# Cached-key scores run head by head between the query projections, and a full 128-row tile in the expert gather

## The chip, the cores and the metric

One core of a Trainium2 chip runs one program. The metric is the device time of one execution in microseconds (us). TensorE is called PE below, VectorE DVE, ScalarE ACT, GpSimd POOL, and SyncE SP; SP issues the loads of the weights.

## What is computed

One inference step of a two-layer decoder trunk, for a prompt of 256 positions and for 8 samples of one position each, with shared weights. Each layer has a mixing part (causal pooling and a gated recurrence), a cross-attention of 4 heads of width 256 into 256 memory tokens, and a channel mixer: a dense SwiGLU in layer 0, the best two of 8 experts in layer 1. All data is float32. The two parts that the change touches are

```
def mem_attend(xn, k, v, wq, wo):
    q = (xn @ wq).reshape(B, T, MEM_HEADS, MEM_HEAD_DIM)
    s = jnp.einsum('bthd,bmhd->bhtm', q, k).astype(jnp.float32) * (MEM_HEAD_DIM ** -0.5)
    p = jax.nn.softmax(s, axis=-1).astype(xn.dtype)
    o = jnp.einsum('bhtm,bmhd->bthd', p, v).reshape(B, T, D_MODEL)
    return o @ wo

def moe(x, router_w, wg, wu, wd):
    ...
    for e in range(N_EXPERTS):
        out = out + combine[:, e:e + 1] * swiglu(xt, wg[e], wu[e], wd[e])
```

The prompt attends to keys and values that are computed in the step from its own memory and written out. Each of the 8 samples attends to cached keys and values of its own, which have to be read from HBM: per layer 8 samples x 4 heads x 256 tokens x 256 numbers for the keys, 8 MB, and as much for the values.

## The kernel before

The five engines run programs written out by hand, kept in step by semaphores. Activations stand with the model dimension on the partitions, prompt and samples side by side: 264 columns, of which 256 are the prompt's and the last 8 the samples'.

**The stream of units.** Weights and cached keys and values come in units of 128 x 1024 numbers, 512 KB each, in the order that `stream_plan` lists. SP loads unit k into slot k modulo 8 of a ring of eight slots, in that order, as soon as the slot is free (L522). A weight unit is split: ACT writes its high part (`high_part`, L993), DVE subtracts it from the raw unit for the low part (`low_part`, L1370) and so frees the slot; three buffers hold split units. A product of weights and activations is three matmuls (high with high, high with low, low with high; L587 to L589), and `project_pair` does two output tiles of 128 with two units, 48 matmuls. Raw units (kinds `kc`, cached keys, and `vc`, cached values) are not split: PE reads them straight from the ring, and a matmul on PE frees their slot (`frees`). In each layer the order is: `in`, `mk`, `mv`, `out`, `kn`, then the 8 query units `mq`, the 16 `kc`, the 16 `vc`, the 8 units `mo` of the attention's output projection.

**The attention** on PE runs in this order: all query projections; the prompt's scores for two halves t of the prompt and two pairs hp of heads (L712); the samples' scores (L724); the transposes of the prompt's probabilities (L735); the prompt's values, eight tiles (L748); the transpose of the samples' probabilities (L754); the samples' values (L764); the transpose of their outputs (L773); then `mo`. A sample has one query column, so the kernel keeps a zeroed array `qz` with eight columns per chunk and sample, of which only the sample's own is filled: a matmul with these 8 columns as its stationary side and a sample's keys as its moving side adds to that sample's row and nothing to the others. Four such matmuls, one per head, write four groups of 32 output partitions (the row of head h and sample b is 32 h + b). The values use an array `pz` of the same kind. DVE takes the maxima (L1545, L1558), ACT the exponentials with their sums, DVE divides (L1551 to L1562) and copies the turned sample probabilities into `pz` (L1572). DVE zeroes `qz` and `pz` in each layer (L1527, L1528). A unit of the caches holds one head of two samples. The sample scores run in four quarters of four units, the four heads of one pair of samples each, and so do the sample values.

**The expert part.** `gather` multiplies the tokens (three tiles of 128, 128 and 8 rows, `TOK`; high and low parts, L848 and L849) with selection matrices to collect each expert's tokens: four times in all, once per pair of experts, 48 matmuls each. `turn_scatter` transposes an expert's selection matrix in the same three pieces (L858).

POOL copies the small outputs, and issues the write-out of the prompt's keys and values (L1829, L1833).

Of the kernel before, what the change touches and what calls it, by code (L numbers as in the profile page):

```python
# [18 lines left out]
ALU = mybir.AluOpType  # L19
# [86 lines left out]
def stream_plan():  # L106
# [22 lines left out]
def bank_plan():  # L129

    out = []
    for l in range(DEPTH):
# [17 lines left out]
        out += [("sc", l, t, hp) for t in range(2) for hp in range(2)]  # L150
        out += [("scs", l)]
        out += [("pt", l, h) for h in range(NH)]
        out += [("pv", l, m) for m in range(KC)]
        out += [("pts", l)]
        out += [("pvs", l)]
# [16 lines left out]
def trunk_kernel(nc, xT, memT, vecs, taps, hists, consts, pool_w, gate_w, router_w, dense, experts,  # L172
# [51 lines left out]
    with ExitStack() as ctx:  # L224
# [63 lines left out]
        STAGE = 3 * NH * NM + NH * MC * TP + KC * TS * TS + NH * MC * TS * TS  # L288
# [17 lines left out]
        pr = take(3 * NH * NM).rearrange("p (t h m) -> p t h m", t=3, h=NH)  # L306
        prs = pr[:, 2, 0, :]
# [98 lines left out]
        kv_written = sem("keys_values_written")  # L406
        qz_ready = sem("sample_queries_ready")
# [6 lines left out]
        mask_ready = sem("mask_ready")  # L414
        route_ready = sem("route_ready")
# [156 lines left out]
        def _(pe):  # L572
# [76 lines left out]
            for l in range(DEPTH):  # L649
# [50 lines left out]
                project("mq", l, xhi, xlo, T, xn_ready, KC * (3 * l + 1))  # L700

                for m in range(KC):
                    wait_read(pe, tiles[key_tile(l, m)])
                    wait_read(pe, tiles[("mq", l, m)])
                for t in range(2):
                    for hp in range(2):
                        n = tiles[("sc", l, t, hp)]
                        b = take_bank(n)
                        for hh in range(2):
                            h = 2 * hp + hh  # L710
                            for c in range(HC):
                                i = mm(b[:, hh * NM:(hh + 1) * NM], q[:, HC * h + c, t * P:(t + 1) * P], kT[:, HC * h + c, :],  # L712
                                       start=(c == 0), stop=(c == HC - 1))
                        full(i, n)

                pe.wait_ge(qz_ready, l + 1)
                n = tiles[("scs", l)]
                b = take_bank(n)
                for bp in range(4):
                    w = [raw_unit(("kc", l, 4 * h + bp)) for h in range(NH)]  # L720
                    for b2 in range(2):
                        for c in range(HC):
                            for h in range(NH):
                                i = mm(b[32 * h:32 * h + TS, 0:NM], qz[:, HC * h + c, 2 * bp + b2, :], w[h][:, 2 * b2 + c, :],  # L724
                                       start=(bp + b2 + c == 0), stop=(bp == 3 and b2 + c == 2))
                                if b2 + c == 2 and bp + h < 6:
                                    frees(i, ("kc", l, 4 * h + bp))
# [1233 lines left out]
```

## Time and profile before

| | |
|---|---|
| median of 3 runs | 1230.55 us (1226.32 to 1233.48) |
| profiled execution, device time | 1220.12 us |
| its span in the profile | 1218.3 us |
| PE busy | 1111.4 us (91%) |
| DVE, ACT busy | 795.8 us, 645.7 us |
| moved by DMA | 273.00 MB, mean 224 GB/s |

Busy time of an engine counts the time in which at least one of its instructions ran. Matmuls overlap on PE, so a matmul's own duration is longer than the step from one to the next. A float32 matmul on raw data is two records in the trace. The granted clock is the share of 2.4 GHz that the throttle let TensorE have; 0.50 is 1.2 GHz. "Idle before" is the time an engine stood still ahead of an instruction, and behind the arrow stands what ended it. All times of the trace count from the start of the span.

### The profile page before, as it was taken

The page shows a single profiled execution, that of the slowest core. Times are in us where ns is not written, and L with a number is a line of the kernel's source. Part 1 is how long each engine was busy: PE and PEld are TensorE (multiplying, and loading weights), DVE is VectorE, ACT ScalarE, POOL GpSimd, SP SyncE. Part 2 cuts the span into 40 slices and gives each one's busy share as a digit, 9 for nine tenths or more (in the row PEclk, how much of TensorE's full clock was granted, in tenths as well). Part 3 has the DMA queues.
Part 4 walks back from the last instruction along what each step waited for, and adds up shares of the span by engine and source line. Part 5 has one row for each costly group of instructions (what it writes and reads, how often), then busy time and mean ns, then how long its engine had stood idle before and what let it go on. Part 6 is the DMA issues. An engine that isn't in the chain of part 4 may idle for free.

```text
span 1218.3 us, 19957 instructions
## 1 busy us (share of the span) xinstructions
PE 1111.4 (91%) x7698; PEld 1027.6 (84%) x7698; DVE 795.8 (65%) x1125; ACT 645.7 (53%) x864; POOL 15.0 (1%) x34
## 2 busy tenths in 40 slices
PE   6998996599999998998966789999999999999995
PEld 5998983399999998998943778998989898989984
DVE  5689641275655555787621464886888688868883
ACT  5675541255433445675421334775767476666762
POOL 0001000000000000010000000000000000000000
PEclk9999998699999999999988876999999999999998
DMA  8443457845555554544647333995989598959861
GB/s 326 155 157 126 164 199 297 313 147 181 185 178 187 174 190 132 171 142 150 223 164 291 137 150 117 347 360 207 346 302 372 192 365 289 361 202 362 306 261 38
DMA packets 64276, 273.00 MB, mean 224 GB/s; under 512 B 7328, under 2 KB 7584, under 8 KB 63552
## 3 DMA queue, kind: packets, MB, share of 16 engines
q1 hardware_dynamic: 62352, 264.33, 61.2%
q0 software_dynamic: 1408, 7.12, 1.6%
q8 instruction: 58, 0.95, 0.3%
q10 hardware_dynamic: 432, 0.38, 0.1%
q14 instruction: 26, 0.21, 0.1%
HBM read 265.83 MB, written 5.98 MB: 223 GB/s over the span
## 4 chain that ended last, share of the span: by engine, by line
PE 71%; DVE 14%; ACT 6%; DMA 4%; issue 3%; SPq 1%; DVEq 0%; ACTq 0%
PE bank L590 10%; PE bank L587 10%; PE bank L592 10%; PE bank L591 10%; PE bank L588 10%; PE bank L589 10%; DMA ring<-dense 4%; DVE wl L1370 3%; PE bank L848 2%; ACT wh L993 2%; DVE rstd L1365 2%; PE bank L615 1%; DVE wl L1621 1%; DVE sq L1381 1%; PE bank L748 1%
## 5 line engine op out<-in xcount | busy, mean ns | idle before, releaser
L1621 DVE TENSOR_TENSOR wl<-ring,wh 128x1408 fp32r<-128x1408 f32 x192 | 310.2, 1624 | 60.4 <-ACT wh L1237 60.2
L1370 DVE TENSOR_TENSOR wl<-ring,wh 128x1024 fp32r<-128x1024 f32 x170 | 206.9, 1223 | 215.7 <-ACT wh L993 215.3
L1237 ACT ACTIVATE wh<-ring 128x1408 fp32r<-128x1408 f32 x189 | 261.0, 1381 | 85.9 <-PE bank L592 85.6
L587 PE MATMUL bank<-xh,wh 128*128 128x264 f32 x928 | 271.6, 293 | 19.0 <-DVE xl L1386 14.7
L993 ACT ACTIVATE wh<-ring 128x1024 fp32r<-128x1024 f32 x170 | 178.8, 1056 | 190.0 <-PE bank L589 143.4
L588 PE MATMUL bank<-xl,wh 128*128 128x264 f32 x928 | 267.3, 288 | 0.0
L589 PE MATMUL bank<-xh,wl 128*128 128x264 f32 x928 | 266.6, 287 | 0.0
L591 PE MATMUL bank<-wh,xl 128*128 128x352 f32 (+4 forms) x736 | 243.9, 331 | 0.0
L587 PEld LDWEIGHTS bank<-xh,wh 128*128 128x128 f32 x928 | 178.6, 192 | 25.6 <-issue 21.4
L588 PEld LDWEIGHTS bank<-xl,wh 128*128 128x128 f32 x928 | 179.1, 193 | 0.0
L589 PEld LDWEIGHTS bank<-xh,wl 128*128 128x128 f32 x928 | 178.3, 192 | 0.0
L590 PE MATMUL bank<-wh,gathered_hi 128*128 128x352 f32 x512 | 167.4, 327 | 2.1 <-DVE xl L1699 1.7
L592 PE MATMUL bank<-wl,gathered_hi 128*128 128x352 f32 x512 | 165.1, 322 | 0.0
L591 PEld LDWEIGHTS bank<-wh,xl 128*128 128x128 f32 x736 | 139.4, 189 | 5.7
L590 PEld LDWEIGHTS bank<-wh,gathered_hi 128*128 128x128 f32 x512 | 96.8, 189 | 3.9 <-issue 2.3
L592 PEld LDWEIGHTS bank<-wl,gathered_hi 128*128 128x128 f32 x512 | 96.7, 189 | 0.0
L587 PE MATMUL bank<-hidden_hi,wh 128*128 128x264 f32 (+1 forms) x304 | 86.6, 285 | 1.6 <-DVE hidden_lo L1398 1.4
L588 PE MATMUL bank<-hidden_lo,wh 128*128 128x264 f32 (+1 forms) x304 | 86.0, 283 | 0.0
L589 PE MATMUL bank<-hidden_hi,wl 128*128 128x264 f32 (+1 forms) x304 | 85.7, 282 | 0.0
L590 PE MATMUL bank<-wh,xh 128*128 128x512 f32 (+3 forms) x224 | 80.0, 357 | 0.0
L592 PE MATMUL bank<-wl,xh 128*128 128x512 f32 (+3 forms) x224 | 79.1, 353 | 0.0
L587 PEld LDWEIGHTS bank<-hidden_hi,wh 128*128 128x128 f32 x304 | 57.2, 188 | 2.4 <-issue 2.3
(217 smaller groups left out, 1370.1 us busy)
## 6 DMA issues: line engine op xcount, KB each, us to landing
ring<-experts SPq DMA_DIRECT2D x192, 704.0 KB, 5.9
ring<-dense SPq DMA_DIRECT2D x234, 512.0 KB, 3.8
o_k<-kv POOLq DMA_DIRECT2D x2, 1024.0 KB, 4.4
o_v<-kv POOLq DMA_DIRECT2D x2, 1024.0 KB, 7.7
x<-xT SPq DMA_DIRECT2D x2, 528.0 KB, 4.9
o_y<-sq SPq DMA_DIRECT2D x4, 264.0 KB, 2.1
gatew<-gate_w POOLq DMA_DIRECT2D x2, 512.0 KB, 8.3
mem<-memT SPq DMA_DIRECT2D x1, 1024.0 KB, 13.3
```

The costliest lines, as they stand in the source:

```text
L587: mm(out, s_hi, m_hi, start=start, stop=False)
L588: mm(out, s_hi, m_lo, start=False, stop=False)
L589: return mm(out, s_lo, m_hi, start=False, stop=stop)
L590: mm(out, s_hi, m_hi, start=start, stop=False)
L591: mm(out, s_lo, m_hi, start=False, stop=False)
L592: return mm(out, s_hi, m_lo, start=False, stop=stop)
L848: mm(out, tokh[0:rows, t, f0:f0 + P], slots, start=(t == 0), stop=False)
L993: A(wh[:, k % NBUF, 0:UNIT], raw(u), ACT.Copy).then_inc(hi_ready, 1)
L1237: A(wh[:, jj % NBUF, :], eraw(jj % ESLOTS), ACT.Copy).then_inc(ehi_ready, 1)
L1365: link(V.reciprocal(rstd[:, buf, 0:width], rms[:, buf, 0:width]))
L1370: V.tensor_tensor(wl[:, k % NBUF, 0:UNIT], raw(u), wh[:, k % NBUF, 0:UNIT].bitcast(F32), ALU.subtract)\
L1621: V.tensor_tensor(wl[:, jj % NBUF, :], eraw(jj % ESLOTS), wh[:, jj % NBUF, :].bitcast(F32), ALU.subtract)\
```

## The change

1. `stream_plan`: the four `kc` units of a head follow the query pair that comes after the head's own, in place of all 16 behind the queries.
2. `sample_scores(h)`: the sample scores run per head. `qz` has 32 columns per chunk and sample (head h's sample b fills column 8 h + b of its 32), and the four matmuls that go to the four partition groups are the four pairs of samples, with one unit each; one bank collects all heads. `qz` now lies where the turned prompt probabilities `pT` are written later. DVE signals `qz_ready` once per head.
3. The prompt's scores run by pair of heads, with head 3's sample scores between the pairs; softmax steps on DVE and ACT follow that order (the semaphore values change with it).
4. The samples' probabilities are turned ahead of the prompt's; the first two quarters of the sample values run between the transposes of the prompt's head pairs, the last two behind the prompt's values. Ahead of the copy of the sample outputs DVE splits one unit of `mo`, where it split three.
5. POOL zeroes `qz` and `pz`, when the mixed parts are ready.
6. `gather` and `turn_scatter` use all 128 rows of the third token tile; POOL zeroes that tile once, in layer 1.

```
@@ stream_plan @@
-        for kind, n in (("in", 12), ("mk", 2 * KEYS_FIRST[l]), ("mv", 8), ("out", 8), ("kn", 2), ("mq", 8)):
+        for kind, n in (("in", 12), ("mk", 2 * KEYS_FIRST[l]), ("mv", 8), ("out", 8), ("kn", 2)):
             add(kind, l, n)
-        for kind in RAW:
-            out += [(kind, l, 4 * h + bp) for bp in range(4) for h in range(NH)]
+        for s in range(NH):
+            out += [("mq", l, 2 * s), ("mq", l, 2 * s + 1)]
+            if s > 0:
+                out += [("kc", l, 4 * (s - 1) + bp) for bp in range(4)]
+        out += [("kc", l, 4 * (NH - 1) + bp) for bp in range(4)]
+        out += [("vc", l, 4 * h + bp) for bp in range(4) for h in range(NH)]
...
@@ buffers @@
-        pT = take(NH * MC * TP).rearrange("p (h c t) -> p h c t", h=NH, c=MC)
-        qz = take(KC * TS * TS).rearrange("p (c b s) -> p c b s", c=KC, b=TS)
+        turned = take(NH * MC * TP)
+        pT = turned.rearrange("p (h c t) -> p h c t", h=NH, c=MC)
+        qz = turned.rearrange("p (c b s) -> p c b s", c=KC, b=TS)
...
@@ PE @@
-                project("mq", l, xhi, xlo, T, xn_ready, KC * (3 * l + 1))
...
+                def sample_scores(h):
+                    pe.wait_ge(qz_ready, NH * l + h + 1)
+                    n = tiles[("scs", l)]
+                    b = take_bank(n) if h == 0 else bank(n)
+                    w = [raw_unit(("kc", l, 4 * h + bp)) for bp in range(4)]
+                    for b2 in range(2):
+                        for c in range(HC):
+                            for bp in range(4):
+                                i = mm(b[32 * bp:32 * bp + 32, 0:NM], qz[:, HC * h + c, 2 * bp + b2, :], w[bp][:, 2 * b2 + c, :],
+                                       start=(h + b2 + c == 0), stop=(h == NH - 1 and b2 + c == 2))
+                                if b2 + c == 2 and h + bp < 6:
+                                    frees(i, ("kc", l, 4 * h + bp))
+                    if h == NH - 1:
+                        full(i, n)
...
+                for s in range(NH):
+                    project_pair("mq", l, s, xhi, xlo, T, xn_ready if s == 0 else None, KC * (3 * l + 1))
+                    if s > 0:
+                        sample_scores(s - 1)
+                prompt_scores(0)
+                sample_scores(NH - 1)
+                prompt_scores(1)
...
+                pe.wait_ge(p_ready, 5 * l + 3)
+                for mc in range(MC):
+                    i = nc.tensor.transpose(b[:, mc * P:(mc + 1) * P], prs[:, mc * P:(mc + 1) * P], ident)
                 full(i, n)
+                for h in (0, 1):
+                    prompt_probs(h)
+                pe.wait_ge(pz_ready, l + 1)
+                sample_values(0)
+                sample_values(1)
+                for h in (2, 3):
+                    prompt_probs(h)
...
+                for m in range(KC):
+                    prompt_values(m)
+                sample_values(2)
+                sample_values(3)
...
-                            slots = gsel[0:rows, t, :, :].rearrange("p b s -> p (b s)")
-                            mm(out, tokh[0:rows, t, f0:f0 + P], slots, start=(t == 0), stop=False)
-                            i = mm(out, tokl[0:rows, t, f0:f0 + P], slots, start=False, stop=(t == 2))
+                            slots = gsel[:, t, :, :].rearrange("p b s -> p (b s)")
+                            mm(out, tokh[:, t, f0:f0 + P], slots, start=(t == 0), stop=False)
+                            i = mm(out, tokl[:, t, f0:f0 + P], slots, start=False, stop=(t == 2))
...
-                for t, (t0, rows) in enumerate(TOK):
-                    i = nc.tensor.transpose(b[:, t0:t0 + rows], wsel[0:rows, t, :], ident[0:rows, 0:rows])
+                for t in range(3):
+                    i = nc.tensor.transpose(b[:, t * P:(t + 1) * P], wsel[:, t, :], ident)
...
@@ ACT @@
+            act.wait_ge(tail_zeroed, 2)
...
@@ DVE @@
-                dve.wait_ge(small_staged, 6 * (l + 1))
-                step(V.memset(qz, 0.0))
-                step(V.memset(pz, 0.0))
...
+                dve.wait_ge(qz_zeroed, l + 1)
                 for c in range(KC):
+                    h = c // HC
                     wait_read(dve, tiles[("mq", l, c)])
-                    step(V.tensor_copy(qz[:, c, :, :].rearrange("p b s -> p (b s)")[:, 0:64:TS + 1], q[:, c, TP:T]))
-                    if c % 2:
+                    step(V.tensor_copy(qz[:, c, :, :].rearrange("p b s -> p (b s)")[:, TS * h:TS * h + 232:33], q[:, c, TP:T]))
+                    if c % HC == HC - 1:
+                        signal(qz_ready)
                         S.upto(behind("mq", l, c, 5, start("mo", l)))
...
-                S.upto(start("mo", l) + 3)
+                S.upto(start("mo", l) + 1)
...
@@ POOL @@
+                pool.wait_ge(mixed_ready, KC * (l + 1))
+                G.memset(turned, 0.0).then_inc(qz_zeroed, 1)
+                G.memset(pz, 0.0).then_inc(pz_zeroed, 1)
...
+            wait_full(pool, tiles[("kn", DEPTH - 1, 1)])
+            G.memset(tokh[:, 2, :].bitcast(F32), 0.0).then_inc(tail_zeroed, 1)
+            G.memset(tokl[:, 2, :].bitcast(F32), 0.0).then_inc(tail_zeroed, 1)
```

For two engines the order now and before, as the program holds it. PE in layer 0, from the last query matmul to the first of `mo`, before (`ring` is a raw unit, `work` holds `qz`, `pz` and the probabilities, `sq` the queries, `kv` the prompt's keys and values, `con` the identity; the shape is that of the output):

```order
L589 MATMUL bank<-xh,wl 128x264
L712 MATMUL bank<-kv,sq 128x256 x16
L724 MATMUL bank<-ring,work 8x256 x64
L735 MATMUL bank<-con,work 128x128 x16
L748 MATMUL bank<-work,kv 128x256 x16
L754 MATMUL bank<-con,work 128x128 x2
L764 MATMUL bank<-ring,work 8x256 x64
L773 MATMUL bank<-con,work 128x128 x2
L587 MATMUL bank<-xh,wh 128x264
```

and the same place in the changed kernel:

```order
L597 MATMUL bank<-xh,wl 128x264
L716 MATMUL bank<-ring,work 32x256 x16
L733 MATMUL bank<-kv,sq 128x256 x8
L716 MATMUL bank<-ring,work 32x256 x16
L733 MATMUL bank<-kv,sq 128x256 x8
L783 MATMUL bank<-con,work 128x128 x2
L745 MATMUL bank<-con,work 128x128 x8
L764 MATMUL bank<-ring,work 8x256 x32
L745 MATMUL bank<-con,work 128x128 x8
L754 MATMUL bank<-work,kv 128x256 x16
L764 MATMUL bank<-ring,work 8x256 x32
L803 MATMUL bank<-con,work 128x128 x2
```

The sample scores (L724, now L716) stand in pieces of one head, two more of which lie further ahead between the query pairs, and the sample values (L764 in both) in two halves around the prompt's values (L748, now L754).

DVE in layer 0, in the changed kernel, from the division of the prompt's first head pair to the copy for the sample values (L1593 to L1597 are the sample's softmax, L1574 and L1575 the maxima of the second head pair, L1608 the copy into `pz`):

```order
L1584 TENSOR_SCALAR work<-work,small 128x256 x2
L1593 TENSOR_REDUCE small<-bank 128x1
L1594 TENSOR_SCALAR small<-small 128x1
L1596 RECIPROCAL small<-small 128x1
L1597 TENSOR_SCALAR work<-work,small 128x256
L1574 TENSOR_REDUCE small<-bank 128x2
L1575 TENSOR_SCALAR small<-small 128x2
L1574 TENSOR_REDUCE small<-bank 128x2
L1575 TENSOR_SCALAR small<-small 128x2
L1608 COPY work<-bank 128x4x8 x2
L1581 RECIPROCAL small<-small 128x2
```

Before, the sample's softmax came behind all divisions of the prompt, and the copy into `pz` behind the eight subtractions that follow the prompt's values.

## Rows read from the trace of the kernel before

**Rows 1.** The page, part 2: granted clock in 40 slices of 30.5 us, in tenths.
```profile
PEclk9999998699999999999988876999999999999998
```
**Rows 2.** Windows: stretch, its length, busy time (and instructions) of PE, PEld, DVE, ACT, POOL, clock, DMA share, GB/s.
```profile
148.40:172.60 24.20, 23.16 (x181) 22.01 (x180) 11.58 (x22) 10.82 (x20) 2.15 (x4) 1.00 0.72 272
172.60:234.17 61.57, 36.91 (x341) 21.91 (x341) 15.58 (x41) 13.74 (x34) 0.00 (x0) 0.81 0.71 263
...
615.50:678.90 63.40, 37.01 (x341) 21.83 (x341) 15.54 (x40) 13.68 (x34) 0.00 (x0) 0.81 0.69 257
...
728.68:745.40 16.72, 15.03 (x48) 11.38 (x49) 6.99 (x17) 2.39 (x4) 0.00 (x0) 0.50 0.25 86
745.40:1218.00 472.60, 452.10 (x2608) 417.05 (x2608) 375.91 (x371) 306.63 (x292) 0.00 (x0) 0.99 0.78 282
```
**Rows 3.** Timeline of PE, layer 0: start, length, instructions, count [idle before <- what ended it].
```profile
179.76 3.64 PE L724 MATMUL bank<-ring,work 128*8 128x256 f32 x64
190.71 3.51 PE L724 MATMUL bank<-ring,work 128*8 128x256 f32 x32 [7.31 <-DMA ring<-dense]
195.76 1.91 PE L724 MATMUL bank<-ring,work 128*8 128x256 f32 x32 [1.54 <-DMA ring<-dense]
...
199.65 7.14 PE L748 MATMUL bank<-work,kv 128*128 128x256 f32 x32
...
208.04 3.64 PE L764 MATMUL bank<-ring,work 128*8 128x256 f32 x64 [1.02 <-DVEq L1348]
218.88 3.60 PE L764 MATMUL bank<-ring,work 128*8 128x256 f32 x32 [7.20 <-DMA ring<-dense]
223.90 3.60 PE L764 MATMUL bank<-ring,work 128*8 128x256 f32 x32 [1.42 <-DMA ring<-dense]
232.37 0.66 PE L773 MATMUL bank<-con,work 128*128 128x128 f32 x2 [4.87 <-DVE work L1582]
```
**Rows 4.** Waits in layer 1 (590 to 682): total us, times, longest us.
```profile
PE bank L764 <- DMA ring<-dense: 9.6, 2, 8.2
PE bank L724 <- DMA ring<-dense: 9.4, 2, 8.0
```
**Rows 5.** Windows of 5 us, columns as in rows 2.
```profile
175.00:180.00 5.00, 5.00 (x31) 4.05 (x33) 3.44 (x11) 2.04 (x8) 0.00 (x0) 1.00 0.00 0
180.00:185.00 5.00, 3.40 (x64) 1.52 (x56) 2.61 (x10) 1.93 (x8) 0.00 (x0) 1.00 0.40 143
...
660.00:665.00 5.00, 1.63 (x16) 0.64 (x20) 0.00 (x0) 0.00 (x0) 0.00 (x0) 0.50 1.02 411
```
**Rows 6.** Line L522, the ring's loads: issue to landing.
```profile
DMA to landing us min/median/max: 3.3/3.8/16.4
```
**Rows 7.** Timelines of ACT and DVE, layer 0, columns as in rows 3.
```profile
229.57 1.06 ACT L993 ACTIVATE wh<-ring 128x1024 fp32r<-128x1024 f32 x1 [1.12 <-DMA ring<-dense]
...
199.25 0.35 DVE L1562 TENSOR_SCALAR work<-work,small 128x256 f32<-128x256 f32 x1
...
230.66 1.23 DVE L1370 TENSOR_TENSOR wl<-ring,wh 128x1024 fp32r<-128x1024 f32 x1 [0.95 <-ACT wh L993]
```
**Rows 8.** Timeline of PE in the second gather, start to the instruction behind it.
```profile
833.76 0.36 PE L848 MATMUL bank<-xh,hidden_hi 128*128 128x256 f32 x1 [0.70 <-DVE x L1693]
...
834.19 0.28 PE L849 MATMUL bank<-xh,hidden_lo 128*128 128x256 f32 x1
834.40 0.38 PE L848 MATMUL bank<-xh,hidden_hi 8*128 8x256 f32 x1
834.63 0.27 PE L849 MATMUL bank<-xh,hidden_lo 8*128 8x256 f32 x1
...
842.50 0.55 PE L877 MATMUL bank<-con,work 128*128 128x128 f32 x3
```
**Rows 9.** Timeline of PE, the first expert's matmuls behind the first gather.
```profile
745.43 0.63 PE L590 MATMUL bank<-wh,gathered_hi 128*128 128x352 f32 x1 [1.72 <-DVE xl L1699]
...
750.26 0.38 PE L591 MATMUL bank<-wh,xl 128*128 128x352 f32 x1
```

More of the change, by code:

```diff
@@ L713, in _, with prompt_probs @@
                                        start=(c == 0), stop=(c == HC - 1))
+                                if hp + hh + t + c == 1 and hp == 1:
+                                    frees(i, ("kc", l, 15))
                         full(i, n)
[L716 to L727, printed above, removed]
-                full(i, n)
-                for h in range(NH):
+                def prompt_probs(h):
                     n = tiles[("pt", l, h)]
@@ L749, in _, with sample_values @@
                     full(i, n)
[L750 to L759 removed]
+                def sample_values(bp):
+                    n = tiles[("pvs", l)]
+                    b = take_bank(n) if bp == 0 else bank(n)
                     w = [raw_unit(("vc", l, 4 * h + bp)) for h in range(NH)]
@@ L1159, in _ @@
                                 i.then_inc(exp_done, 1)
-                n = tiles[("scs", l)]
-                act.wait_ge(max_ready, 5 * l + 5)
-                read(A(prs, bank(n)[:, 0:NM], ACT.Exp, bias=nmx[:, 8:9], scale=HD ** -0.5, accum_out=sm[:, 8:9]), n)
+                    if hp == 0:
+                        n = tiles[("scs", l)]
+                        act.wait_ge(max_ready, 5 * l + 3)
+                        read(A(prs, bank(n)[:, 0:NM], ACT.Exp, bias=nmx[:, 8:9], scale=HD ** -0.5, accum_out=sm[:, 8:9]), n)
                 for h in range(NH):
@@ new lines, in normalize @@
+                def normalize(t, hp):
+                    j = 4 * t + 2 * hp
+                    dve.wait_ge(exp_done, 4 * l + 2 * hp + t + 1)
+                    wait_read(dve, tiles[("sc", l, t, hp)])
+                    link(V.reciprocal(rs[:, j:j + 2], sm[:, j:j + 2]))
+                    for hh in range(2):
+                        h = 2 * hp + hh
+                        step(V.tensor_scalar(pr[:, t, h, :], pr[:, t, h, :], rs[:, j + hh:j + hh + 1], None, ALU.mult))
+                    signal(p_ready)
@@ L1556, in _ @@
+                for t in range(2):
+                    top(t, 0)
+                for t in range(2):
+                    normalize(t, 0)
                 n = tiles[("scs", l)]
@@ L1578, in _ @@
                 signal(pz_ready)
-                S.upto(start("mo", l) + 3)
+                for t in range(2):
+                    normalize(t, 1)
+                for m in range(KC):
+                    n = tiles[("pv", l, m)]
+                    dve.wait_ge(oh_ready, KC * l + m + 1)
+                    read(V.tensor_tensor(xlo[:, m, 0:TP], bank(n)[:, 0:TP], xhi[:, m, 0:TP].bitcast(F32), ALU.subtract), n)
+                S.upto(start("mo", l) + 1)
                 n = tiles[("pvs", l)]
```

95 lines of the change are left out of this document (40 added, 55 removed).

## The prediction

> **What bounds the kernel now.** I read the page's slices first: the granted TensorE clock is full almost everywhere and dips in three places [rows 1], the seventh and eighth slice (the attention of layer 0), the twenty-first to twenty-third (that of layer 1), and the two behind, where tokens are routed and gathered. Outside these places PE is near 90% busy, so what PE does in them sets the time. Then the busy time by stretch [rows 2]: from the first prompt score to the first output projection, layer 0 takes 61.57 us of which PE works 36.91, layer 1 takes 63.40 with 37.01. The four query projections ahead of it fill their 24.20 us (23.16 busy, so 5.8 us for a pair of tiles of 48 matmuls, 0.121 each), and in them the DMA moves only 272 GB/s.
>
> The timeline of PE shows where the idle time lies [rows 3]. The sample scores (L724) run their first half in 3.64 us, then PE waits 7.31 us for a load of the ring, runs a quarter, waits 1.54, runs the last. The sample values (L764) do the same: 3.64 us, then waits of 7.20 and 1.42. At the end there is a wait of 4.87 us until DVE has copied the sample outputs. In layer 1 the waits on loads in the same places sum to 9.4 and 9.6 us [rows 4]. Why the loads are late is in the windows [rows 5]: between 175 and 180 us, while PE does prompt scores, the DMA moves nothing. The ring has eight slots, all of them hold raw cache keys, and none is given back before the sample scores, which come last. When they come, half of sixteen units are there and the other half has to stream, at up to 411 GB/s, with PE standing still. The waits also cost clock: it is 1.00 while the first 64 narrow matmuls run and 0.50 in the window 660 to 665, after the wait, so that a quarter takes 3.5 to 3.6 us in place of 1.9 [rows 3, 5].
>
> **The attention, part by part.** The change puts each head's four key units behind the next query pair, so the sample scores of one head (16 matmuls, 32 records, 1.9 us at full clock by the last row of scores) free four slots in the middle of the projections. The loads then run beside 23 us of projections. The sample values are split around the prompt's, which take 7.14 us [rows 3], so that the second half of the value cache loads beside them.
>
> Removed in layer 0: waits 7.31 + 1.54 + 7.20 + 1.42 = 17.5 us, and the half-clock excess of the quarters behind them, (3.51 - 1.85) + 2 x (3.60 - 1.82) = 5.2 us [rows 3]; 22.7 us. Layer 1: 9.4 + 9.6 = 19.0 [rows 4], with the same excess 24.3. Together 47.0 us.
>
> New waits, per layer. (a) The query units of the last pair now stand in the queue behind the second head's keys, in slots that only the first head's scores give back. From there a load lands in 3.8 us [rows 6], two units more lie ahead of it (512 KB at 411 GB/s is 1.28 us each), then ACT (1.06) and DVE (1.23) split it [rows 7], with some 0.3 us of hand-over: 9.0 us, while PE has a pair and one head's scores to do, 5.8 + 1.9 = 7.7. A wait of 1.3. If the queue moves only the 272 GB/s of that stretch (1.93 us a unit), because the prompt's keys and values are written out at the same time, it is 2.6. Bounds 0 (the loads are on time) and about 4 (both ends slip, and the second unit too); I take 2.5, near the busy queue. (b) The sample probabilities need DVE (reduce, exp on ACT, scale): 2.0 us from the last score at 197.6 to the end of the scale at 199.6 [rows 3, 7]. Behind that, DVE now takes two maxima of the second head pair before it may copy the turned probabilities. PE has the second pair's prompt scores and some transposes to cover it. Today PE waits 1.02 us on DVE in that place [rows 3]. Bounds are 0 and 3 (the softmax wholly bare, and 1 us of copy and hand-over); I take 1.3, near the row of today, so 0.3 on top. (c) The last four value units load in slots that the second quarter frees; eight loads in 3.8 + 7 x 1.28 = 12.8 us, while PE has 1.9 + 1.0 + 7.1 + 1.9 = 11.9 from the first quarter's end: 1.3 us with its hand-over, bounds 0 and 3. (d) The tail stays. The first output-projection unit uses the slot of the third quarter of the values, as before, so the 4.87 us (and what follows it) is not won: DVE must split that unit before it copies the sample outputs. It waits for one unit now and not three, but the matmuls ahead are faster, so less lies in front of it; I take 0.5 more, between -3 and 2. Sum of (a) to (d): 2.5 + 0.3 + 1.3 + 0.5 = 4.6 a layer, 9.2 in all.
>
> The two memsets of 512 columns leave DVE for POOL, which waits for the mixed parts and is idle there; cover: the output projection and the key pair that lie between the mixing and the first query copy, over 20 us. Nothing on the path. POOL's key write-out stands behind them, but waits for the last keys anyway. The score matmuls have 32 stationary columns where they had 8. I put the longer weight load at nothing: one of 128 columns already hides behind each matmul of a query pair.
>
> Each change between full and narrow matmuls costs. A full matmul of 256 columns needs 0.117 us (0.121 x 256/264). In the gather at full clock the first 8-row one starts 0.21 after its neighbour, and the second 0.23 after that; a group of six needs 1.09 us (8.74/8) against 0.70 [rows 8]. That is at most 0.38 for one trip into the other shape and back. The attention makes two such trips per layer now and will make six: eight more, 2.9 us at 0.36. The Trainium skill's TensorEngine Tiling, section Key Properties, says that a change of tiling mode drains the engine. This speaks against the attention's new order and for the gather's; the trace agrees, and priced without it the sum would be 2.9 us better in the attention.
>
> Net attention: 47.0 - 9.2 - 2.9 = 34.9 us.
>
> **The gather.** Its last third of tokens is eight rows; the change runs it as 128 with zeros. Three gathers at full clock take 8.74 us each from the first matmul to the one behind [rows 8]; 48 matmuls at 0.117 and a start of 0.1 are 5.7. PE is on the path there (95% busy between 745 and 1218) [rows 2], so 3 x 3.0 = 9.0 us. The first gather is different: it runs from 728.68 to 743.7 (745.43 less the wait of 1.72) wholly at 1.2 GHz [rows 2, 9], and the expert matmuls behind it start at that clock, 0.30 us a step for 16 steps, until at 750.26 they shorten [rows 9]. Without holes 48 steps of 0.30 x 256/352 = 0.22 are 10.5 us at 1.2 GHz: 4.5 won. If the clock rises behind a like unbroken run (745.43 to 750.26 there), 22 steps pass at 0.22 and 26 at 0.117, 7.9 us: 7.1 won, and 16 x (0.30 - 0.16, the same at full clock) = 2.2 behind it, so 9.3. I take 9.3, since the unbroken expert row is the nearest; 4.5 is the other end. The eight transposes of the 8-row piece make trips of the same sort, 0 to 0.36 each less a longer transpose; I take 1.0 for all. The zeroing is POOL's and lies far ahead. Sum 19.3 us.
>
> **The sum.** 34.9 + 19.3 = 54.2 us off. The profiled execution, span 1218.3 and 1220.1 in all, would take 1165.9. The runs shown have a median of 1230.55, 10.4 above it, so I take the difference off the median: 1176 us.
>
> **The rivals.** *A, the loads stay the bound* (they only wait elsewhere). Layer 0's stretch from 148.4 on must pass eleven key and query units, 5.8 MB, beside the outputs that share the 6.6 MB moved there today [rows 2]; and each is held back by a slot. If every head waits 3 us, the attention gains some 17 less: 1193. For it: eight slots for six units per head. Against: the DMA stands idle at 175 to 180 us. The Trainium skill's DMA: Bandwidth & Descriptors, section Specifications, puts the HBM limit at about 358 GB/s per core; by it a unit takes 1.46 us, (a) and (c) grow by some 1.6 a layer, and the time would be 1179. The trace does not agree: 411 GB/s over 5 us [rows 5], so I keep its rate.
>
> *B, slower: the narrow matmuls take the clock.* Between projections they may not hold 2.4 GHz, and then the whole stage from the first query pair on runs at 1.2. PE's work there is 23.2 + 4 x 1.9 + 36.9 less the 5.2 of excess and the old scores' 7.2, some 55 us; doubled it is 110, against 86 now, and the tail of 6 comes on top: 30 us a layer lost, 60 - 19 = 41 in all, 1271. It decides when over half of that stage falls to 1.2 GHz. Against it: the clock is 1.00 in 180 to 185, with x64 narrow records in it [rows 5]; it fell in waits.
>
> *C, the holes in the gather are not the 8 rows'.* Then the second part gives nothing: 1196. Against: in every group the wide steps stand at the 8-row matmuls and directly behind. *D, the first gather stays at 1.2 GHz*: 1181; inside the range.
>
> **Chances.** Forecast with D as its lower variant 0.70; A 0.14; C 0.05; both A and C or a softmax chain that takes the place of the loads (no gain beyond 0.5%, which is about what a measurement here can tell) 0.05; B 0.06. So faster 0.89, same 0.05, slower 0.06. The range runs from 1154 (no new wait at all, 9 + 3 us more, and a session with 10 us less, as the profiled one) to 1200 (A or C).
>
> **What would show it.** After: PE waits on loads in L724's and L764's places of under 3 us each in a layer; DMA busy between the scores; granted clock 1.00 from the first query pair to the last values; about 35 us from the first prompt score to the output projection; a wait before the last query pair; gathers of some 5.7 us, the first of some 8. The prediction is wrong if the query pairs stand apart by over 4 us, if the clock is 0.50 in them, or if the gather's steps keep their 0.2.

## The result, and the profile after

The changed kernel takes 1163.72 us (median of 4 runs, 1162.4 to 1165.84), the kernel before 1228.43 beside it (1220.62 to 1233.48): ratio 0.948, 95% interval 0.944 to 0.952. The forecast was 1176, the range 1154 to 1200. The profiled execution takes 1164.83 us with a span of 1163.0, 55.3 less than the span of before. One execution of the kernel before, beside the first experiments, took 6041.79 us, is counted as slow, and stands in no comparison below.

The page of the changed kernel, the row of [rows 1]:

```profile
PEclk8999999899999999999999869999999999999998
```

A slice is 29.1 us here. Layer 0's attention keeps a dip in one slice (the eighth, 204 to 233 us, the end of it) where there were two, layer 1's none, and the output projection behind it one (the twenty-third, 640 to 669), where the two had three, and the slice of the routing and the first gather (the twenty-fourth) one where there were two. The first slice, the start, is at 8 where it was at 9.

Windows of the changed kernel (columns as in [rows 2]): from layer 0's second query pair to the first prompt score, from there to the first output projection, and parts of them:

```profile
156.38:182.30 25.92, 23.72 (x241) 20.60 (x241) 6.82 (x13) 7.67 (x12) 0.89 (x2) 1.00 0.99 371
182.30:217.00 34.70, 26.55 (x249) 18.59 (x245) 13.60 (x39) 12.85 (x33) 0.00 (x0) 0.96 0.88 323
...
175.00:180.00 5.00, 5.00 (x44) 5.00 (x43) 0.90 (x4) 0.39 (x1) 0.00 (x0) 1.00 0.88 319
...
210.00:215.00 5.00, 1.69 (x32) 0.69 (x24) 1.37 (x2) 2.11 (x2) 0.00 (x0) 0.91 0.90 334
215.00:220.00 5.00, 3.67 (x16) 3.34 (x17) 2.91 (x5) 1.06 (x1) 0.00 (x0) 0.50 1.02 403
```

The stretch that took 61.57 us [rows 2] takes 34.70; about 35 was forecast. The five microseconds from 175 in which the DMA moved nothing [rows 5] now move 319 GB/s. In layer 0 the clock stays at 2.4 GHz until the wait ahead of the output projection. The timeline of PE in layer 0 shows where the waits have gone (columns as in [rows 3]; L716 are sample scores, L733 prompt scores, L764 sample values, L754 prompt values, L803 the transpose of the sample outputs, L595 the first matmul of a projection):

```profile
162.36 1.93 PE L716 MATMUL bank<-ring,work 128*32 128x256 f32 x32
...
170.81 1.93 PE L716 MATMUL bank<-ring,work 128*32 128x256 f32 x32 [0.49 <-DMA ring<-dense]
174.44 0.36 PE L595 MATMUL bank<-xh,wh 128*128 128x264 f32 x1 [1.70 <-DVE wl L1402]
...
180.44 1.93 PE L716 MATMUL bank<-ring,work 128*32 128x256 f32 x32
182.30 3.72 PE L733 MATMUL bank<-kv,sq 128*128 128x256 f32 x16
185.98 1.93 PE L716 MATMUL bank<-ring,work 128*32 128x256 f32 x32
...
193.09 1.91 PE L764 MATMUL bank<-ring,work 128*8 128x256 f32 x32 [0.44 <-DVEq L1380]
197.28 1.91 PE L764 MATMUL bank<-ring,work 128*8 128x256 f32 x32 [2.27 <-DMA ring<-dense]
...
200.05 7.07 PE L754 MATMUL bank<-work,kv 128*128 128x256 f32 x32
207.05 1.91 PE L764 MATMUL bank<-ring,work 128*8 128x256 f32 x32
209.78 1.91 PE L764 MATMUL bank<-ring,work 128*8 128x256 f32 x32 [0.81 <-DMA ring<-dense]
215.34 0.66 PE L803 MATMUL bank<-con,work 128*128 128x128 f32 x2 [3.65 <-DVE work L1624]
```

In place of the waits of 7.31, 1.54, 7.20 and 1.42 us [rows 3] stand waits of 0.49, 1.70, 2.27 and 0.81, and in layer 0 every quarter runs at full clock (1.9 us). Layer 1 has the same pattern except in one place: its second quarter of the sample values runs at half clock behind its wait, and takes 3.54 us.

```profile
620.31 3.54 PE L764 MATMUL bank<-ring,work 128*8 128x256 f32 x32 [2.21 <-DMA ring<-dense]
```

The waits of PE in layer 1 (570 to 642 us; total, times, longest), where two lines of 9.6 and 9.4 us stood [rows 4]:

```profile
PE bank L803 <- DVE work L1624: 4.7, 1, 4.7
PE bank L764 <- DMA ring<-dense: 2.2, 1, 2.2
PE bank L595 <- DVE wl L1402: 1.9, 2, 1.7
```

From the start of the second query pair to the first output projection, layer 0 takes 60.61 us where it took 79.85, layer 1 61.75 where it took 81.72: 39.2 us off.

The gather, in the timeline of PE: the second gather's first steps, of which [rows 8] show the counterpart:

```profile
789.76 0.36 PE L878 MATMUL bank<-xh,hidden_hi 128*128 128x256 f32 x1 [0.70 <-DVE x L1735]
789.96 0.28 PE L879 MATMUL bank<-xh,hidden_lo 128*128 128x256 f32 x1
790.08 0.28 PE L878 MATMUL bank<-xh,hidden_hi 128*128 128x256 f32 x1
790.20 0.28 PE L879 MATMUL bank<-xh,hidden_lo 128*128 128x256 f32 x1
```

Behind the first step of 0.20 us every step is 0.12 now; the wide ones have gone. From its first step to its last the gather takes 5.64 us where it took 8.53. The first gather takes 8.15 in place of 14.62. The wide steps have gone there too, and the clock rises in it, as these windows show:

```profile
693.00:697.00 4.00, 3.88 (x18) 3.91 (x19) 3.86 (x10) 0.60 (x1) 0.00 (x0) 0.50 0.40 130
697.00:700.00 3.00, 3.00 (x21) 3.00 (x21) 1.44 (x4) 0.60 (x1) 0.00 (x0) 0.71 0.87 308
700.00:703.00 3.00, 1.55 (x14) 1.34 (x12) 1.47 (x3) 1.20 (x2) 0.00 (x0) 1.00 0.00 0
```

From the start of the first gather to the end of the span it is 469.9 us against 489.6: 19.7 off. The rest of the span gives 3.6 back: 2.1 at the start (the clock is 0.71 from 20 to 25 us where it was 1.00), 1.8 between layer 1's attention and the first gather (the output projection's first 11.1 us run at 0.73 in place of 0.85, which is some 1.3 of it); 0.2 is won between the attention of layer 0 and that of layer 1. 39.2 + 19.7 - 3.6 = 55.3.

### The profile page after: what moved, and what is told of

It reads as the page before. It is cut to its first block, busy times and chain, and to the rows that moved or that the text cites. A ratio compares the mean times of both kernels' runs of the same rounds, so it can differ in the third digit from the quotient of the medians.

```text
span 1163.0 us, 19968 instructions
## 1 busy us (share of the span) xinstructions
PE 1088.9 (94%) x7698; PEld 1022.9 (88%) x7698; DVE 794.7 (68%) x1121; ACT 646.4 (56%) x864; POOL 21.5 (2%) x40
## 4 chain that ended last, share of the span: by engine, by line
PE 71%; DVE 15%; ACT 7%; DMA 3%; issue 3%; SPq 0%; DVEq 0%; ACTq 0%
PE bank L598 10%; PE bank L595 10%; PE bank L600 10%; PE bank L599 10%; PE bank L596 10%; PE bank L597 10%; DVE wl L1402 4%; DMA ring<-dense 3%; ACT wh L1023 2%; PE bank L623 2%; DVE rstd L1397 2%; DVE wl L1663 2%; DVE sq L1413 1%; PE bank L754 1%; PE bank L878 1%
## 5 line engine op out<-in xcount | busy, mean ns | idle before, releaser
L595 PE MATMUL bank<-xh,wh 128*128 128x264 f32 x928 | 272.9, 294 | 21.3 <-DVE xl L1418 13.7
L595 PEld LDWEIGHTS bank<-xh,wh 128*128 128x128 f32 x928 | 179.6, 194 | 29.6 <-issue 25.1
L595 PE MATMUL bank<-hidden_hi,wh 128*128 128x264 f32 (+1 forms) x304 | 86.7, 285 | 1.6 <-DVE hidden_lo L1430 1.4
L595 PEld LDWEIGHTS bank<-hidden_hi,wh 128*128 128x128 f32 x304 | 57.2, 188 | 2.4 <-issue 2.3
```

The costliest lines, as they stand in the source:

```text
L595: mm(out, s_hi, m_hi, start=start, stop=False)
```

## Experiments

**Each half by itself.** The first run has the changed attention and the gather of before, the second the reverse. The edit of the first, against the changed kernel, shortened:

```
-    mm(out, tokh[:, t, f0:f0 + P], slots, ...)
+    mm(out, tokh[0:rows, t, f0:f0 + P], slots, ...)
...
-    i = nc.tensor.transpose(b[:, t * P:(t + 1) * P], wsel[:, t, :], ident)
+    i = nc.tensor.transpose(b[:, t0:t0 + rows], wsel[0:rows, t, :], ident[0:rows, 0:rows])
```

> The change without its part 6: the gather and the transposes keep the 8-row tile, the attention is the new one. If the two parts add up as the stages of the profile say, the attention stages give 39 us by the profiles (19 in layer 0, 20 in layer 1), so a ratio of 0.965 to 0.972, and the first gather takes 15 us again at 1.2 GHz. Rival: the gain of the attention is partly clock or luck of the start, then the ratio is above 0.975.

> The kernel before with part 6 alone. By the stages of the profile the gathers and what stands behind them give 18 us: ratio 0.983 to 0.988; each later gather 5.7 us from its first matmul to the instruction behind it, the first one 8 us with the clock rising in it. Rival: the later gathers are hidden behind DVE's splitting, then only the first one counts, some 9 us, ratio 0.992.

The attention alone takes 1182.17 us (1178.97 to 1189.54), ratio 0.960 (0.956 to 0.963); the gather alone 1204.69 (1204.07 to 1206.27), ratio 0.979 (0.976 to 0.982). Both gain more than I had expected, and together more than both at once: 47.4 + 24.8 = 72 us against 64.7 (taken up at the end). A second thing stood out: in the trace of the first run, the second gather takes 12.83 us, not 8.5. The clock leaves it on its way, with PE busy all the time:

```profile
795.00:800.00 5.00, 4.29 (x23) 3.22 (x21) 4.35 (x10) 0.60 (x1) 0.00 (x0) 0.96 0.94 295
800.00:805.00 5.00, 5.00 (x17) 3.68 (x16) 1.38 (x2) 0.60 (x1) 0.00 (x0) 0.50 0.17 66
805.00:810.00 5.00, 5.00 (x18) 3.88 (x17) 0.69 (x1) 0.60 (x1) 0.00 (x0) 0.50 0.00 0
810.00:815.00 5.00, 5.00 (x20) 4.10 (x20) 2.02 (x5) 1.87 (x3) 0.00 (x0) 0.67 0.00 0
```

The profile of before that the prediction read has no such gather. This is taken up below, with the kernel before under the trace again.

**What the eight rows cost: their number, or the change of shape?** The changed kernel with the last token tile cut to 64 and to 32 rows (the rest are zeros, so what is computed stays the same), and with 8 rows in pairs, so that two groups of six share one trip into the other shape (shortened; first the 64 rows, then the pairs):

```
+    rows = P if t < 2 else 64
-    slots = gsel[:, t, :, :]...
+    slots = gsel[0:rows, t, :, :]...
...
```

```
-    for t, (t0, rows) in enumerate(TOK):
+    for k, t in enumerate(((0, 1, 2), (2, 0, 1))[c]):
+        rows = TOK[t][1]
```

> The changed kernel, but the third token tile enters the gather with 64 rows (8 of tokens and 56 of zeros) in place of 128. Theory 1, the holes are the price of changing between a matmul over all rows of the array and one over a part of them: 64 rows cost what 8 did, a group of six 1.07 us at full clock, and the first gather stays at 1.2 GHz for 15 us; the time is 13 us above the changed kernel. Theory 2, the holes come from how few rows are filled: at 64 rows they are about half, or gone.

> The same with 32 rows. Theory 1: again 1.07 us a group and 13 us above the changed kernel. Theory 2: holes between those of 8 and of 64 rows, nearer those of 8.

> The changed kernel with 8 rows in the gather again, but in every second group the 8-row pair comes first, so that two such pairs stand side by side: half the changes between full and narrow rows, with the same matmuls. Theory 1, the price is per change of shape: two groups of six take 1.77 us at full clock in place of 2.18, a later gather 7.1 us in place of 8.5. Theory 2, the price is in the 8-row matmuls themselves: 2.18 and 8.5 as before. Both leave open whether the clock rises in the first gather.

They take 1180.52 us with 64 rows, 1188.40 with 32 and 1176.55 with the pairs, one execution each; the first two stand 17 and 25 us above the changed kernel's median, where 13 was expected. With 64 rows the later gathers take 8.51, 8.54 and 8.54 us, with 32 rows 8.53 in the two where the clock holds and 12.71 in the other, with 8 rows in pairs 7.18 each. The timeline of PE in the second gather with 64 rows:

```profile
796.07 0.38 PE L879 MATMUL bank<-xh,hidden_hi 64*128 64x256 f32 x1
796.29 0.28 PE L880 MATMUL bank<-xh,hidden_lo 64*128 64x256 f32 x1
796.49 0.39 PE L879 MATMUL bank<-xh,hidden_hi 128*128 128x256 f32 x1
796.72 0.27 PE L880 MATMUL bank<-xh,hidden_lo 128*128 128x256 f32 x1
```

and with the pairs of 8 rows:

```profile
796.31 0.38 PE L879 MATMUL bank<-xh,hidden_hi 8*128 8x256 f32 x1
796.53 0.28 PE L880 MATMUL bank<-xh,hidden_lo 8*128 8x256 f32 x1
796.65 0.28 PE L879 MATMUL bank<-xh,hidden_hi 8*128 8x256 f32 x1
796.77 0.28 PE L880 MATMUL bank<-xh,hidden_lo 8*128 8x256 f32 x1
796.97 0.39 PE L879 MATMUL bank<-xh,hidden_hi 128*128 128x256 f32 x1
```

A matmul behind the first of a new shape starts 0.22 us after it, and the first one back starts 0.20 after its neighbour, with 8, 32 and 64 rows alike; inside the pair an 8-row matmul steps by 0.12 like a full one. A group of six costs 1.09 us with one trip, 0.90 with half a trip, 0.71 with none: 0.38 a trip. So at full clock the price goes with the changes of shape and not with the number of rows; the pairs halve it. Their first gather stays at 1.2 GHz to its end (12.54 us), while with full tiles the clock rises in it.

**The attention taken apart.** One kernel has the scores early and all sample values behind the prompt's, the other the values split and all sample scores behind the prompt's, with all query units ahead of the keys in the stream, as before (both edits shortened):

```
-    sample_values(0)
-    sample_values(1)
...
-    sample_values(2)
-    sample_values(3)
+    for bp in range(4):
+        sample_values(bp)
```

```
-    if s > 0:
-        sample_scores(s - 1)
...
-    sample_scores(NH - 1)
...
+    for h in range(NH):
+        sample_scores(h)
```

> The changed kernel, but the sample values run all four quarters behind the prompt's values, as before; the scores stay head by head between the query pairs. Theory, each half of the attention's gain is the loads of its own half: the 8.6 and 9.6 us of waits on loads at the values and their half-clock quarters come back, less what the loads win by an earlier start, so 7 to 12 us a layer, a ratio to the kernel before of 0.960 to 0.970 (changed kernel 0.948). Rival: the loads are one queue, and with the keys out of the way early the values' loads are no longer late; then the ratio stays within 0.003 of 0.948.

> The changed kernel, but its query units come first in the stream and all sample scores run behind the prompt's scores, as before; the values stay split around the prompt's. Theory: the waits of 8.9 and 9.4 us at the scores come back with a half-clock quarter, 8 to 12 us a layer: ratio 0.960 to 0.970. Rival, the queue as a whole is the bound: the time lost at the scores is won back later, and the ratio stays within 0.005 of 0.948.

Scores early: 1179.97 us (1177.74 to 1180.95), ratio 0.961 (0.954 to 0.968). Values split: 1191.67 (1189.53 to 1194.91), ratio 0.972 (0.965 to 0.979), a little above the 0.960 to 0.970 expected. The timeline of PE with the scores early, at the second half of the sample values:

```profile
212.09 3.59 PE L764 MATMUL bank<-ring,work 128*8 128x256 f32 x32 [6.92 <-DMA ring<-dense]
217.12 1.91 PE L764 MATMUL bank<-ring,work 128*8 128x256 f32 x32 [1.44 <-DMA ring<-dense]
```

and with the values split, at the second half of the sample scores (L713 there):

```profile
190.32 3.64 PE L713 MATMUL bank<-ring,work 128*32 128x256 f32 x32 [7.70 <-DMA ring<-dense]
195.36 1.93 PE L713 MATMUL bank<-ring,work 128*32 128x256 f32 x32 [1.40 <-DMA ring<-dense]
```

Whichever of the two stays in one piece keeps its waits of 7 and 1.4 us. From the second query pair to the output projection the scores alone win 11.2 us in layer 0 and 12.7 in layer 1, the values alone 4.3 and 8.8, both 19.2 and 20.0. In layer 0 the two alone give 15.5 and together 19.2: the values split alone still find their first two quarters late there.

**One place earlier still.** Head 3's scores ahead of all prompt scores, half of the prompt's values ahead of the third quarter and half between the third and the fourth (shortened):

```
-    prompt_scores(0)
     sample_scores(NH - 1)
+    prompt_scores(0)
...
-    for m in range(KC):
+    for m in range(4):
         prompt_values(m)
     sample_values(2)
+    for m in range(4, KC):
+        prompt_values(m)
     sample_values(3)
```

> A version to beat the change: the last head's sample scores come directly behind the third's, the sample softmax ahead of the prompt's, the turned sample probabilities between the two prompt score pairs, and the third quarter of the sample values in the middle of the prompt's values, so that slots are free some 4 us earlier. Theory, the waits left in the attention (2.2 us at the second quarter of the values, 0.8 at the fourth, 3.7 to 4.7 before the output's transpose) come from slots freed late: 3 to 6 us a layer less, ratio to the changed kernel 0.990 to 0.995. Rival, the DMA is now full in the attention (share 0.88 over 150 to 217 us): the same waits move to another place, within 0.002 of the changed kernel.

1164.58 us (1163.93 to 1167.63), ratio 0.949 (0.943 to 0.956): as the changed kernel, where 3 to 6 us a layer had been hoped for. The waits move. In layer 0 the tail falls to 1.26 us, but head 3's scores now wait 3.69 for their keys and the third quarter of the values 2.22; ahead of the first quarter stand 1.81 us for which the profile names no load. From the second query pair to the output projection layer 0 takes 65.57 us for the changed kernel's 60.61, and layer 1 61.25 for 61.75; the stages behind each of the two win 4.3 us back (1.7 and 2.6). I took the waits for a full DMA (357 GB/s from 156 to 188 us), and tried that next.

**Less to move in the attention.** The write-out of the prompt's keys and values, and layer 1's gate weights behind it, held back until the sample outputs are copied, in the changed kernel and in the one with the earlier places:

```
+    wait_read(pool, tiles[("pvs", l)])
     pool.dma_start(o_k[l], kT).then_inc(kv_written, 16)
```

> The changed kernel, with the write-out of keys and values (2.1 MB a layer, and in layer 0 0.8 MB of gate and pool weights behind it) held back until the attention's sample outputs are copied. Theory: transfers now bound the attention (over 320 GB/s in it), so taking 2.1 to 2.9 MB away, 5 to 7 us of transfer a layer, shortens the waits on the ring's loads (0.5 + 2.3 + 0.8 us in layer 0, 2.2 in layer 1, and part of the wait of 1.7 before the last query pair): 3 to 5 us a layer at the most, 6 to 9 in all, ratio to the changed kernel 0.992 to 0.995. Rival: the loads are late because their slots come free late; then the waits stay and the ratio is within 0.002 of 1.

> The kernel with scores and values one place earlier, with the write-out of keys and values held back in the same way. Theory: there the loads wait for the transfers still more (3.7 + 1.8 + 2.2 us in layer 0, 1.8 + 1.8 + 2.1 in layer 1), so it gains 4 to 6 us a layer, and comes out below the changed kernel: 1153 to 1158 us. Rival (slots): as before, within 2 us of the changed kernel.

1166.15 us (1164.43 to 1169.17) and 1165.57 (1164.28 to 1169.44), ratios 0.950 (0.943 to 0.957) for both: nothing gained, and the theory that fewer bytes shorten the waits falls; for the second run 1153 to 1158 us had been expected. Windows of the first, the last of which has the bounds of the window 156.38 to 182.30 of the changed kernel above:

```profile
160.00:163.00 3.00, 3.00 (x42) 1.93 (x41) 0.29 (x3) 0.39 (x1) 0.00 (x0) 1.00 0.03 8
163.00:170.00 7.00, 6.03 (x57) 5.70 (x59) 0.00 (x0) 0.00 (x0) 0.00 (x0) 1.00 0.84 287
156.38:182.30 25.92, 23.26 (x234) 19.98 (x233) 5.08 (x10) 6.58 (x10) 0.00 (x0) 1.00 0.76 277
```

And the waits of PE in it, layer 0 (150 to 217 us; total, times, longest):

```profile
PE bank L764 <- DMA ring<-dense: 3.4, 1, 3.4
PE bank L595 <- DVE wl L1402: 2.0, 2, 1.7
PE bank L716 <- DMA ring<-dense: 1.0, 1, 1.0
```

In the same window the DMA now moves 277 GB/s where it moved 371 with the change, and the same waits stand there (1.7 ahead of the last query pair; L716 and L764 no less). From the second query pair to the output projection layer 0 takes 63.95 us, 3.3 more than in the changed kernel, and layer 1 60.95, 0.8 less, so no gain in the attention was lost again elsewhere. At 160 to 163 the DMA is idle: eight units lie in the ring, and the next load can go out only when the first head's scores end, at 162.4. The write-out had filled a time that the ring couldn't use. The longest wait on loads in layer 0 of the changed kernel, ahead of the second quarter of the sample values, shows what its end hangs on. SP issues its four loads when head 3's scores end (185.98 + 1.93):

```profile
188.04 1.91 SPq L530 DMA_DIRECT2D ring<-dense  x4
```

They land 5.3 to 7.5 us after their issue, behind four loads that left from 182.5 on, and PE goes on at 197.28: 9.2 us from the slots to the matmuls. With the write-out held back it is 10.3 (186.61 to 196.96). So the end of this wait is set by the moment at which four slots come back together and by the ring's own loads, and not by the write-out. No run here has more slots or smaller units, which would tell the first two apart.

**The 10 us between the profiled execution and the median.** The kernel before, unchanged, once more under the trace, twice:

> The kernel before once more, for its trace: the profiled execution that the prediction read took 1220.1 us, most others 1229. Theory: in an ordinary execution one of the three later gathers loses the clock on its way, as it did in the two kernels with narrow rows in the gather whose traces show it (12.8 and 12.7 us in place of 8.5), with 9 to 10 us more in all; then this trace shows one such gather if it takes about 1229, and none if it takes about 1220. Rival: the 10 us lie elsewhere (start, loads, the attention).

> The kernel before a third time under the trace, alone. The two executions traced so far took 1220.1 and 1220.8 us with a mean granted clock of 0.954 and 0.955, and show three later gathers of 8.5 us; executions of 1227 to 1238 us have 0.948 to 0.936, and clock times span is nearly the same in all of them (1219.0 x 0.955 = 1164, 1227.4 x 0.948 = 1164, 1233.3 x 0.941 = 1161), so that what they take more is time at half clock. Theory: it lies in a later gather, one that loses the clock on its way (12.7 us in place of 8.5, and the expert's first steps behind it): in an execution of 1227 us or more the trace shows one such gather, in one of 1235 two. Rival: the half clock lies elsewhere (the start, the attention, the loads of the first layers), and the three gathers stay at 8.5 us. If it takes about 1220 once more, neither is told apart.

The first took 1220.83 us and shows 8.53, 8.54 and 8.53 us for the three later gathers, the second 1233.83 and 12.94, 8.53 and 12.78. Windows of the second at the first of these gathers:

```profile
835.00:838.00 3.00, 3.00 (x16) 2.38 (x16) 2.32 (x8) 0.60 (x1) 0.00 (x0) 0.88 0.93 332
838.00:841.00 3.00, 3.00 (x11) 2.18 (x10) 0.55 (x1) 0.15 (x1) 0.00 (x0) 0.50 0.18 71
...
847.00:850.00 3.00, 3.00 (x11) 2.36 (x11) 0.99 (x2) 1.09 (x2) 0.00 (x0) 0.50 0.00 0
850.00:853.00 3.00, 3.00 (x14) 2.57 (x14) 1.02 (x4) 0.95 (x1) 0.00 (x0) 0.84 0.00 0
```

The clock falls in the gather's third group and comes back in the expert's matmuls behind it. From the start of that gather to the next it is 120.55 us against 114.76 in the profile that the prediction read, and from the fourth gather to the end 161.8 against 154.7: 5.8 + 7.0 = 12.8 of the 13.7 by which the two executions differ. So the theory holds in the one long execution that was traced: its later gathers lost the clock twice, at some 6 to 7 us each. An execution of 1226 to 1230 us, the commonest, was not traced; one lost gather would fit it.

## Why the prediction was right, and where it was off

**The sum held.** "The profiled execution, span 1218.3 and 1220.1 in all, would take 1165.9": its counterpart takes 1164.8. That the two lie 1.1 apart is luck in part: the attention won 4.3 us more than was forecast, and the rest of the span, which the sum left out, gave 3.6 back.

**The step that failed** is the one behind it: "The runs shown have a median of 1230.55, 10.4 above it, so I take the difference off the median: 1176 us." It takes the 10.4 us for something that the change leaves alone. The last run shows what it very likely is: later gathers at half clock. The change takes this away too: a later gather without changes of shape kept the full clock in every trace (21 in seven traces, 5.63 to 5.64 us each), while with one trip a group the clock was lost in 4 of 18 (six traces). The times of the runs agree: with the gather alone changed they lie between 1204.07 and 1206.27, those of the kernel before between 1220 and 1239. The changed kernel's median stands 1.1 us below its profiled execution, and not 10.4 above it. The profile of before was 10 us faster than the median because it lacked something, and that had to be found before the offset was carried over.

**The attention: 39.2 us where 34.9 was forecast.** The removal of 47.0 (its terms add to 46.9) came nearly as worked out: the four long waits are gone, and so are the half-clock quarters of layer 0, but in layer 1 one quarter of the values stays at half clock, so the clock was not 1.00 to the last values there. The terms against it were put at 4.6 a layer. (a), the last query pair: 2.5 forecast; 0.49 + 1.70 = 2.2 measured (1.9 in layer 1). (b), the sample probabilities: 0.3 more than the 1.02 of before; the wait is 0.44, so 0.6 less. (c), the last quarter of the values: 1.3; measured 0.81, and none in layer 1. But the second quarter waits 2.27 (2.2 in layer 1), which the text doesn't name: its four units need the slots of head 3's scores, leave at 188.04 behind the first quarter's, and PE goes on at 197.28, 9.2 us later. Four loads by the prediction's own rates would be 3.8 + 3 x 1.28 = 7.6 us; a sum of this kind, made for the last four units, belonged here as well. And from 180 to 200 us the DMA moved 313 to 355 GB/s in windows of 5 us, not the 411 behind the 1.28. (d), the tail: 0.5 more than 4.87; it is 1.2 less in layer 0, at 3.65, and 4.74 in layer 1. In layer 0 these sum to 0.49 + 1.70 - 0.58 + 2.27 + 0.81 - 1.22 = 3.5 in place of 4.6. Layer 0 beats its forecast by another 1.5 us or so. 0.7 of it is a wait that the sum left out and that has gone, ahead of the prompt's first scores, where PE stood until ACT had written the last queries:

```profile
172.68 7.14 PE L712 MATMUL bank<-kv,sq 128*128 128x256 f32 x32 [0.68 <-ACT sq L1143]
```

With the change the same scores (L733 at 182.30) follow a head's sample scores without a wait. The remaining 0.8 is not assigned to a row.

The price of the eight extra trips into the narrow shape was taken from the gather, 0.36 each; the gather's kernels give 0.38. In the attention the first narrow matmul stands 0.21 behind its neighbour, and the second full one behind it 0.22 after the first, as the gather's do; what a whole trip costs there was not measured by itself. The longer weight load (32 columns) is hidden; 32 records take 1.93 us, as the 1.91 of before. The Trainium skill's TensorEngine Tiling, section Key Properties, says that a change of the tiling mode drains TensorE; the trace agrees, with steps in the gather of 0.20 to 0.22 in place of 0.12 at each change.

**The gather: 19.7 us where 19.3 was forecast.** The steps lost their holes and the first gather's clock rose, as worked out. From the first gather to the second 8.4 (9.3 for it was taken, by the rise of the clock, which came); the three stretches behind it 3.4, 3.7 and 4.2, for 3.0 each and 1.0 for the transposes of all.

**The rivals.** A (the loads stay the bound) fell in its size: no wait on a load is over 2.3 us. What remains is of its kind, though, and in the runs with earlier places and with less to move the waits moved or stayed, and nothing was gained. The Trainium skill's DMA: Bandwidth & Descriptors, section Specifications, has some 358 GB/s per core; the changed kernel moves 371 over 25.92 us and 403 over 5, so the trace doesn't agree here, on one core running alone. B (narrow matmuls between projections take the clock) fell: 1.00 over layer 0's whole query stage, with 96 narrow records in it. C fell by the steps of the changed gather, and the three gather kernels show why. D fell: the first gather's clock rose.

## What to carry to other kernels

Where PE waits for streamed raw data late in a stage, look at when the slots are given back, not only at the rate: consuming a quarter of the data in the middle of dense work starts the next loads earlier, and taking other bytes away from a queue that waited for slots gained nothing here. The last partial tile of rows between full ones cost by the number of changes of shape, not by its rows: pad it, or run its pieces side by side. And when the profiled execution is faster than the median, find the difference first; it may be the thing that the change removes.

## What was not expected of the hardware

In the kernels with changes of shape in the gather, the clock fell from 2.4 to 1.2 GHz in the middle of it, with PE busy 3.00 of 3.00 us, and stayed there to the gather's end: in two of three later gathers of one execution of the kernel before and in none of two other executions of the same program. The same happened in the second gather of the kernel with the attention alone (12.83 us) and with 32 rows (12.7), and not with 64 rows or with the pairs (one execution each). In the execution shown above it came back in the dense expert matmuls behind. That the changes of shape are what loses the clock is not shown beyond the counts of 4 in 18 and 0 in 21. What tells an execution that loses it from one that doesn't was not found. That the two halves of the change gain 72 us apart and 64.7 together seems to be the same thing. In the traces they don't gain more apart: against the span of 1218.3 the gather alone (1202.6) gains 15.7 us, and the attention alone (1187.7) gains 30.6, or 36.7 when the 6.1 us of its one lost gather are taken off (120.87 us from the second gather to the third, where the kernel before took 114.76); 52.4 in all, against 55.3 for both at once. So the surplus of the medians would lie in how many gathers lost the clock in the executions compared; the medians' own intervals, some 4 us either way on each gain, also cover a good part of it.
